# Four GpSimd operations for each weight panel's low part, in place of one

## The reference

```python
def swiglu(h, w_gu, w_down):
    gu = h @ w_gu
    g, u = jnp.split(gu, 2, axis=-1)
    return (jax.nn.silu(g) * u) @ w_down
...
mod = (c_act @ w_mod[l] + b_mod[l]).reshape(c.shape[0], N_MOD, D_MODEL)
h = modulate(x, g_norm[l, 0], mod[:, 0], mod[:, 1])
x = x + 0.5 * mod[:, 2][:, None, :] * swiglu(h, w_ffn1_gu[l], w_ffn1_down[l])
```

## Time and profile before

| | |
|---|---|
| median of 3 runs | 3996.78 us (3995.74 to 3997.22) |
| the profiled execution | 4000.66 us, its span 3998.5 us |
| granted TensorE clock, mean | 0.971 |
| busy | TensorE 94%, VectorE 54%, GpSimd 37%, ScalarE 36% |
| DMA | 441.73 MB, 110 GB/s over the span |

### The profile page before, as it was taken

How to read it: one execution, slowest core, us unless ns; L and a number is a source line. 1 busy time by engine, 2 the same in 40 slices (tenths; PEclk the granted TensorE clock), 3 DMA queues, 4 the chain that set the end, 5 groups by cost and what they waited for, 6 DMA issues and landing times.

```text
span 3998.5 us, 66438 instructions
## 1 busy us (share of the span) xinstructions
PE 3777.7 (94%) x26315; PEld 3147.4 (79%) x26315; DVE 2168.0 (54%) x3408; ACT 1428.1 (36%) x2032; POOL 1489.6 (37%) x503
## 2 busy tenths in 40 slices
PE   6999999999999978999999998999999999989998
PEld 5888778888888867888776666877779888878887
DVE  5444676444644578755554555678766534434332
ACT  3322353322422244332234442342425434435332
POOL 1443333443334423334431002244447743334442
PEclk9999999999999998999999999899999999999998
DMA  5454524454444434335220002234444432212321
GB/s 183 149 153 131 154 85 148 129 166 134 150 136 158 135 88 117 106 126 168 93 71 15 14 23 81 78 121 124 130 130 148 155 100 62 77 53 84 95 92 55
DMA packets 560084, 441.73 MB, mean 110 GB/s; under 512 B 60396, under 2 KB 558077, under 8 KB 559613
## 3 DMA queue, kind: packets, MB, share of 16 engines
q1 hardware_dynamic: 559869, 438.67, 35.8%
HBM read 431.58 MB, written 2.83 MB: 109 GB/s over the span
## 4 chain that ended last, share of the span: by engine, by line
PE 68%; DVE 13%; issue 11%; ACT 3%; POOL 2%; DMA 1%; SPq 1%; DVEq 0%; ACTq 0%; POOLq 0%
PE ps_all L2370 19%; PE ps_all L2372 19%; PE ps_all L2371 19%; DVE acc L3085 5%; PE ps_all L2065 1%; DMA g_raw<-in_w_mod_dram 1%; ACT w_hi L1482 1%; PE ps_all L2355 1%; POOL w_lo L915 1%; PE ps_all L2085 1%; DVE acc L3087 1%; POOL w_lo L920 1%; DVE squares L2789 1%; PE ps_all L2326 1%; PE ps_all L2350 1%
## 5 line engine op out<-in xcount | busy, mean ns | idle before, releaser
L920 POOL TENSOR_TENSOR w_lo<-raw,w_hi 128x2048 fp32r<-128x2048 f32 (+4 forms) x284 | 1197.5, 4218 | 2259.5 <-ACT w_hi L1482 2150.5
L2370 PE MATMUL ps_all<-h_hi,w_hi 128*128 128x512 f32 (+1 forms) x2680 | 1056.3, 394 | 26.9 <-POOL w_lo L920 14.8
L2371 PE MATMUL ps_all<-h_lo,w_hi 128*128 128x512 f32 (+1 forms) x2680 | 1042.3, 389 | 0.0
L2372 PE MATMUL ps_all<-h_hi,w_lo 128*128 128x512 f32 (+1 forms) x2680 | 1042.0, 389 | 0.0
L1482 ACT ACTIVATE w_hi<-raw 128x2048 fp32r<-128x2048 f32 (+4 forms) x278 | 472.6, 1700 | 1342.5 <-PE ps_all L2372 1262.1
L2370 PEld LDWEIGHTS ps_all<-h_hi,w_hi 128*128 128x128 f32 x2680 | 512.0, 191 | 135.2 <-issue 20.9
L3085 DVE SCALAR_TENSOR_TENSOR acc<-g_raw,c_col,acc 128x256 f32<-128x256 f32 x1104 | 616.8, 627 | 1.7
L2372 PEld LDWEIGHTS ps_all<-h_hi,w_lo 128*128 128x128 f32 x2680 | 510.8, 191 | 104.9
L2371 PEld LDWEIGHTS ps_all<-h_lo,w_hi 128*128 128x128 f32 x2680 | 511.8, 191 | 99.6
L2370 PE MATMUL ps_all<-hid_hi,w_hi 128*128 128x512 f32 (+1 forms) x1282 | 481.7, 376 | 21.5 <-DVE hid_lo L3200 14.1
L2372 PE MATMUL ps_all<-hid_hi,w_lo 128*128 128x512 f32 (+1 forms) x1282 | 473.8, 370 | 0.0
(11 more groups left out here) (425 smaller groups left out, 5248.5 us busy)
## 6 DMA issues: line engine op xcount, KB each, us to landing
raw<-in_w_ffn_gu_dram SPq DMA_DIRECT2D x88, 1024.0 KB, 5.1
g_raw<-in_w_mod_dram SPq DMA_DIRECT2D x72, 1024.0 KB, 5.1
raw<-in_ffn_w_in_dram SPq DMA_DIRECT2D x66, 1024.0 KB, 5.1
g_raw<-in_ada_w_dram SPq DMA_DIRECT2D x48, 1024.0 KB, 5.3
raw<-in_w_ffn_down_dram SPq DMA_DIRECT2D x32, 768.0 KB, 4.7
raw<-in_w_ffn_down_dram SPq DMA_DIRECT2D x32, 640.0 KB, 4.3
raw<-in_ffn_w_out_dram SPq DMA_DIRECT2D x24, 768.0 KB, 4.7
raw<-in_ffn_w_out_dram SPq DMA_DIRECT2D x24, 640.0 KB, 4.3
```

The costliest lines, as they stand in the source:

```text
L920: nc.gpsimd.tensor_tensor(v(w_lo), v(raw), v(w_hi).bitcast(F32), ALU.subtract).then_inc(sem["w_split_lo"], 1)
L2370: nc.tensor.matmul(o, whi, mhi, start=first, stop=False)
L2371: nc.tensor.matmul(o, whi, mlo, start=False, stop=False)
L2372: return nc.tensor.matmul(o, wlo, mhi, start=False, stop=last)
```

## The change

`split_lo` makes the low part of a panel in four operations along the contraction. The edges are `nk * t // 4`, so 8 chunks make 2, 2, 2, 2; 12 make 3, 3, 3, 3; 10 make 2, 3, 2, 3; 3 make three operations of one chunk and 2 make two. The wait for `w_split_hi` stands ahead of the first, and only the last increments `w_split_lo`. The context's feed-forward leaves `split_lo` above these lines and stays as it is.

```diff
             pool.wait_ge(sem["w_split_hi"], number(st, i, j) + 1)
-            v = lambda t: w_view(t, j % 2, st["shapes"][j])
-            nc.gpsimd.tensor_tensor(v(w_lo), v(raw), v(w_hi).bitcast(F32), ALU.subtract).then_inc(sem["w_split_lo"], 1)
+            nk = st["shapes"][j][0]
+            edges = [nk * t // 4 for t in range(5)]
+            for first, end in zip(edges, edges[1:]):
+                if first < end:
+                    v = lambda t: w_view(t, j % 2, st["shapes"][j])[:, first:end, :]
+                    ins = nc.gpsimd.tensor_tensor(v(w_lo), v(raw), v(w_hi).bitcast(F32), ALU.subtract)
+            ins.then_inc(sem["w_split_lo"], 1)
```

## The result

The changed kernel took 3943.72 us (median of 4 runs, 3939.27 to 3947.30), against 3997.00 for the kernel before (4 runs, 3995.74 to 4002.72): a ratio of 0.9861, 95% interval 0.9848 to 0.9873. That is 53 us less. I had said 3972, with a range down to 3956: right side, size too small by half.

The account below looks back on a forecast made before the run. TensorE, busy 3777.7 of 3998.5 us, was taken as the bound, with only some 221 us idle to win. Gains of 30.1 less losses of 5.5 gave 24.6 off the median 3996.78: 3972, own range 3960 to 3982, full range 3956 to 3993.

Parts of the forecast that it names:

- gate 9.3: Feed-forward with convolution: TensorE's waits for ScalarE's SiLU (L1605), 12.4 us less 3.1 in the context's part, vanish: 9.3 us.
- its last steps 2.5 + 2.8: TensorE's waits for the last dot-product step: 2.5 us gained at 2793, 2.1 and 0.7 behind two 1536 panels.
- last steps elsewhere (1409 and 1624): TensorE's waits for the last dot-product step: 3.1 us gained each, cut to 2.0 at 1409.
- adding L3092 (L2120): L2120 waits, three with w_lo in them, steps and adding held one by one: 3.1 of 30.5 us gained.
- squares: Presum of squares, held 4.65 us with TensorE waiting 2.24, becomes hidden; with two small ones 3.1 us gained.
- latent attention's end and rotated key: Held diagonal tile at the latent attention's end, 3.5 of 4.4 us gained, and 0.7 for the rotated key before it.
- diagonal tiles: Attention's diagonal-tile waits, 20.6 us, stay, as many held steps follow in VectorE's queue: change 0, bounds -2 and +2.
- w_lo itself and sharing, hid_lo: TensorE's waits for w_lo lose 3.3 us, sharing 1.6, the neighbourhood attention's end 0.6: 5.5; waits for hid_lo 0.
- the held last step: VectorE's last dot-product step, held by w_lo, falls from 4.60 to 1.46 us: 3.1 each where TensorE waits for it.
- the waits on L3085: TensorE's waits for VectorE's dot-product steps, said to go down by some 10 us.
- slower rival: Two: VectorE not let in between parts, 4008 us, chance 0.05; every part wins against the stream anew, 4077, 0.04.
- its lower end: Range's lower bound, 3956 us: no losses (5.5), and half of what is left standing in the 20.9 us of last-step waits.

Follow-up runs that it names:

- e5: Changed kernel with three added 128x768 VectorE reductions ahead of the gated convolution, making the gate late with nothing held; 3960.6 us, 0.9910 of the kernel before.
- e6: Kernel before with one added matmul in TensorE's wait for the gate, each pass but the first of the feed-forward with convolution; 3998.4 us, ratio 1.0008.
- e10: Changed kernel with four added VectorE reductions ahead of the gated convolution instead of the three of e5; 3970.5 us, 0.9931 of the kernel before.
- e13: Changed kernel with TensorE waiting, ahead of each plain feed-forward up panel, until ScalarE has read the gate; 4193.3 us, 1.0493 of the kernel before.
- e15: Changed kernel with the wait of e13 and three added matmuls into a free bank ahead of it; 4119.5 us, 1.0310 of the kernel before.
- e14: Changed kernel with the wait of e13 placed two of the eight rows later in the up panel; 3989.4 us, 0.9977 of the kernel before.

## Why the prediction was wrong

Step by step, sizes from the profiled executions:

| step of the prediction | booked us | measured us |
|---|---|---|
| feed-forward with convolution: gate 9.3, its last steps 2.5 + 2.8 | -14.6 | -27.3 |
| last steps elsewhere (1409 and 1624) | -5.1 | -9.5 |
| adding L3092 (L2120) | -3.1 | -5.1 |
| squares | -3.1 | -2.9 |
| latent attention's end and rotated key | -4.2 | -4.9 |
| diagonal tiles | 0 | -2.8 |
| w_lo itself and sharing, hid_lo | +5.5 | +2.6 |
| TensorE's clock outside the convolution | not in the sum | -6.6 |
| sum | -24.6 | -56.5 of -57.9 |

**The step that failed** is "They are 12.4 us less one of 3.1 in the context's part, which isn't changed: 9.3 us." The waits fell by exactly 9.3 us, so the number of the view was right, and it was the wrong price. I took TensorE's visible waits for what the held step costs. In this stage the step lies in a ring of VectorE and ScalarE that sets the pass, and the price is ring less TensorE's work at full clock, 1.9 us in every pass, seen or not. Six whole passes gave 11.9 us, the way to the first SiLU 5.0 and the stretch with the stage's last steps 10.3. e5, e6 and e10 show it for the passes: their length follows VectorE's work and not TensorE's clock.

**A term that was missing**, and the largest, is TensorE's busy time, which I had left as it was: it fell by 18.7 us, of the 33.3 that the profiled executions gave beyond my 24.6. In the stage with convolution it is nearly the whole surplus: idle time fell there by 15.3 us, about what I had booked, and busy time by 12.1. Of these 12.1 some 5.6 lie in the six passes, where the lower clock had filled the ring's slack, and 6.5 in the rest of the stage (3.6 of them between the waits of 2.92 and 5.21 us, where the clock rose from 0.92 to 1.00). Outside that stage busy time fell by 6.6 us. That waits can take clock with them is shown by e13 against e15; that the 6.5 and the 6.6 us came from the waits that went is not. Of the 6.6 some 1.7 and 1.8 us lie in stretches whose waits shrank (behind the first mixer, and around the squares), but 3.4 behind a wait for the diagonal tiles that hardly changed (7.1 to 6.9 us), and 3.9 went the other way in the last layer (3494 to 3755 us before). This part stays open.

**Sized too small:** the last steps outside. I had priced the held last step, 4.60 to 1.46, but the same change also frees what stands ahead of the stream (1409), and at 1624 the stream now ends before the next w_lo begins (it starts at 1599.05, the last step ends at about 1599.0), so that the hold is not shortened but gone: 7.11 to 2.12 us. For the diagonal tiles I had said that a stream of held steps gains nothing; they gained 2.8, just past my bound of 2. For the waits on L3085 I had said some 10 less: they fell by 17.6, of which 9.5 here.

**Right:** VectorE is let in after each part; a part that shares takes 1.4 to 1.5 us; no step over 1.6 us (1.57); the losses where TensorE waits for w_lo, 5.5 booked and 5.8 measured in the earlier trace rows's line (3.0 without the new one of 2.82 us in the convolution's stage, where a late w_lo took the place of a wait that went); hid_lo nothing. Neither slower rival came about. The Trainium skill says in SBUF — State Buffer, section SBUF: two separate sides, that VectorE and GpSimd take their common pair of ports by a lock held for the whole instruction. The runs agree: the longest dot-product step went from 4.88 to 1.57 us with the size of GpSimd's instruction, 2.68 us with two parts.

The range failed because it was built from the same visible waits: its lower end added half of what I left standing in the earlier trace rows, and nothing for passes in which TensorE has slack without a wait, or for TensorE's busy time.

## What to carry to other kernels

Before pricing a held instruction by the waits behind it, measure the pass from one fixed instruction to the next and ask whether it changes with TensorE's clock: if it doesn't, another ring sets it, and the gain is that ring less TensorE's work at full clock. An operation that blocks another engine is best cut in two or four even if its sum grows, and the consumer should then wait for the part it needs; here that gave another 9 us with four parts and 20 with eight, and only then did the smallest parts pay. Where TensorE sets the pace, waits of 2.4 to 4.6 us cost 2.1 us each on top of their length (e13), and waits of up to 1.7 us no clock (e14), so the longest ones are to be shortened first.

## What the runs showed of the hardware

**The granted clock behind a wait.** TensorE's waits for ScalarE's gate, in all traces kept here: behind those under 1 us it never fell (44 cases); of 1.0 to 1.5 us it fell behind 2 of 10, of 1.5 to 1.8 behind 1 of 41, of 1.8 to 2.4 behind 13 of 19 and over 2.4 behind 56 of 61. A fall to the lower level (1.2 GHz) behind a wait of 2.19 us left 48 matmuls in place of 55 in the 12.5 us that followed, a mean of 0.86; behind 4.33 us it was 0.90 and 0.92 over the pass. Equal waits (1.81 us, twice, before the change) had different outcomes, 0.87 and 1.00. The Trainium skill, TensorE: Matmul & The Clock Gate, Part 1, says that the clock follows the engine's recent activity, and that the stretches it is judged by run free of the kernel; that fits with equal waits ending differently, which no run here isolates.

**Added work can be free and more.** 132 additional matmuls in e15 made the kernel 73.8 us faster than the same waits empty. In the kernel before, where TensorE had slack in the ring, ten of them changed nothing that can be measured (ratio 1.0008, 0.9999 to 1.0017).
